# Second mixer of a two-layer language model: gated linear attention with fewer meta outputs, states inside the projection loop, and a head norm by chunk

## What is computed

```python
def gla_chunk(state, q, k, v, log_a):
    cum = jnp.cumsum(log_a, axis=2)
    diff = cum[:, :, :, None, :] - cum[:, :, None, :, :]
    decay = jnp.where(causal[:, :, None], jnp.exp(jnp.minimum(diff, 0.0)), 0.0)
    scores = jnp.einsum('bhtk,bhsk,bhtsk->bhts', q, k, decay)
    out = jnp.einsum('bhts,bhsv->bhtv', scores, v) + jnp.einsum('bhtk,bhkv->bhtv', q * jnp.exp(cum), state)
    last = cum[:, :, -1:, :]
    new_state = state * jnp.exp(last)[:, :, 0, :, None] + jnp.einsum('bhsk,bhsv->bhkv', k * jnp.exp(last - cum), v)
    return new_state, out

def gla_mix(p, g_up, g_b, head_gain):
    q, k, v, gd, r = jnp.split(p, [kw, 2 * kw, 2 * kw + vw, 2 * kw + vw + GLA_LORA], axis=-1)
    log_a = jax.nn.log_sigmoid((gd @ g_up + g_b).astype(f32)) / GLA_TAU   # GLA_TAU = 16
    ...   # 4 heads, keys 128 wide, values 256 wide; one chunk of 16 meta tokens, then 4 chunks of 64
    o = o * lax.rsqrt(jnp.mean(o * o, axis=-1, keepdims=True) + NORM_EPS)
    o = o.reshape(B, T, vw) * head_gain.astype(f32) * jax.nn.silu(r.astype(f32))
    return o.astype(p.dtype)
...
    p = rms_norm(h, o_norm[i]) @ o_w_in[i]
    h = h + gla_mix(p, ...) @ o_w_out[i]
```

## Time and profile before

| What | us |
|---|---|
| Median of 3 runs (lowest, highest) | 939.5 (937.5, 945.36) |
| The profiled execution: its time | 939.7 |
| Its span in the trace | 938.2 |
| PE busy (share) | 807.9 (86%) |
| DVE busy (share) | 342.3 (36%) |
| ACT busy (share) | 195.1 (21%) |
| Mean granted clock of PE | 0.947 |

### The profile page before, as it was taken

How to read it: one execution, slowest core, us unless ns; L and a number is a source line. 1 busy time by engine, 2 the same in 40 slices (tenths; PEclk the granted TensorE clock), 3 DMA queues, 4 the chain that set the end, 5 groups by cost and what they waited for, 6 DMA issues and landing times.

```text
span 938.2 us, 17020 instructions
## 1 busy us (share of the span) xinstructions
PE 807.9 (86%) x7630; PEld 541.1 (58%) x7630; DVE 342.3 (36%) x716; ACT 195.1 (21%) x387; POOL 12.8 (1%) x62
## 2 busy tenths in 40 slices
PE   8999898789999987899889999987899987667765
PEld 6778677764675546455526877866356543334421
DVE  4472756431343332332234065424425221112122
ACT  4552137220500000000012251303031100000002
POOL 5000000000000000000000000000000000000000
PEclk9999899899899999999999999997889998889889
DMA  9451003119649999999998412030564999999994
GB/s 268 131 150 47 1 2 134 50 30 424 266 154 423 420 421 420 368 422 419 422 383 290 158 53 89 1 143 38 222 266 170 422 420 422 420 421 419 421 421 166
DMA packets 61093, 242.06 MB, mean 258 GB/s; under 512 B 9414, under 2 KB 33084, under 8 KB 36060
## 3 DMA queue, kind: packets, MB, share of 16 engines
q1 hardware_dynamic: 60956, 240.94, 65.0%
q10 hardware_dynamic: 64, 0.02, 0.0%
HBM read 239.90 MB, written 1.05 MB: 257 GB/s over the span
## 4 chain that ended last, share of the span: by engine, by line
PE 63%; DMA 24%; DVE 6%; ACT 3%; issue 2%; SPq 1%; PEldq 0%; POOL 0%; DVEq 0%; POOLq 0%
PE ps L1245 11%; DMA M<-in_m_w_down_dram 10%; DMA M<-in_m_w_up_dram 10%; PE ps L790 8%; PE ps L1095 7%; PE ps L989 6%; PE ps L1059 5%; DMA M<-in_m_w_gate_dram 4%; PE ps L1135 4%; PE ps L1072 2%; PE ps L938 2%; PE ps L746 2%; PE ps L1224 1%; PE ps L904 1%; PE ps L1001 1%
## 5 line engine op out<-in xcount | busy, mean ns | idle before, releaser
L1095 PE MATMUL ps<-M 128*32 128x256 f32 x2048 | 127.7, 405 | 45.1 <-DMA M<-in_m_w_gate_dram 33.1
L1095 PEld LDWEIGHTS ps<-M 128*32 128x32 f32 x2048 | 73.0, 117 | 109.4 <-issue 64.2
L1245 PE MATMUL ps<-M 128*128 128x272 f32 (+3 forms) x464 | 108.7, 394 | 1.0 <-DVE M L1349 1.0
L1245 PEld LDWEIGHTS ps<-M 128*128 128x128 f32 (+2 forms) x464 | 82.7, 181 | 23.9 <-issue 4.5
L790 PE MATMUL ps<-M 128*128 128x272 f32 x352 | 88.1, 405 | 1.0 <-DVE M L1349 1.0
L1059 PE MATMUL ps<-M 128*128 128x128 f32 x688 | 81.9, 280 | 3.7 <-DVE M L1727 3.7
L1059 PEld LDWEIGHTS ps<-M 128*128 128x128 f32 x688 | 80.0, 196 | 5.5 <-DVE M L1727 4.6
L1659 DVE TENSOR_TENSOR H<-H,ps 128x512 f32<-128x512 f32 x68 | 46.8, 688 | 87.8 <-PE ps L1072 87.5
L1072 PE MATMUL ps<-M 128*128 128x512 f32 x136 | 68.3, 624 | 9.9 <-DVE H L1662 6.8
L1135 PE MATMUL ps<-M 128*32 128x512 f32 x512 | 65.5, 595 | 13.2 <-DMA M<-in_m_w_down_dram 7.5
L790 PEld LDWEIGHTS ps<-M 128*128 128x128 f32 x352 | 66.5, 193 | 15.9 <-issue 2.0
(11 more groups left out here) (340 smaller groups left out, 864.0 us busy)
## 6 DMA issues: line engine op xcount, KB each, us to landing
M<-in_m_w_gate_dram SPq DMA_DIRECT2D x32, 2048.0 KB, 18.9
M<-in_m_w_up_dram SPq DMA_DIRECT2D x32, 2048.0 KB, 23.5
M<-in_m_w_down_dram SPq DMA_DIRECT2D x32, 2048.0 KB, 25.9
M<-in_o_w_in_dram SPq DMA_DIRECT2D x12, 1024.0 KB, 5.7
M<-in_e_w_in_dram SPq DMA_DIRECT2D x11, 1024.0 KB, 5.2
M<-in_e_w_out_dram SPq DMA_DIRECT2D x1, 4096.0 KB, 14.0
M<-in_o_w_out_dram SPq DMA_DIRECT2D x1, 4096.0 KB, 18.8
H<-in_x_dram SPq DMA_DIRECT2D x2, 512.0 KB, 4.2
```

What stands on the lines that cost most here:

```text
L1095: ins = pe.matmul(ps[32 * e:32 * e + 32, 3 * x, 0:FF], xgT[q % 2][:, k, 32 * e:32 * e + 32], gu_w[UNIT_SLOT[y][u]][:, e, k, :], start=(k = ...
L1245: ins = pe.matmul(ps[rows, unit % 4, 0:n], lhs(k), rhs(k), start=(k == 0), stop=(k == KD - 1))
```

## The change

- **Projection.** The q and r units no longer compute the meta columns (256 instead of 272); k and the decay input keep them. The four value units for the meta tokens become one unit ahead of the other value units: for each of the 8 input blocks four matmuls of 32 weight columns (`xnO` columns 32 to 63) into four strips of 32 partitions, one per value group. It needs the groups 5 to 8 loaded, and ACT evacuates it with four copies of 32 partitions. The 32 rows of `Vo` ahead of them are zeroed. 26 units instead of 29.
- **No meta outputs.** Pairs, exponents, masks and outputs run over chunks 1 to 4; `decayed_rows` over chunks 0 to 3, those that feed a state.
- **States in the loop.** `state_step` stands after units 17, 19, 21 and 23, two steps each; DVE updates them after `pt_add(1)` to `pt_add(4)`. The first state is a copy. The pair rounds stand after units 15, 16, 18, 20, 22, 24 and 25, the exponents after the evacuations 13, 14, 16, 18, 20 and 22.
- **Decay.** min and subtraction are one DVE pass; the factor 1/16 goes into the scale of each Exp.
- **Gate.** ACT multiplies the gain into the gate at its evacuation, a second pass; DVE's eight passes over it go.
- **Head norm by chunk.** ACT squares a chunk's output out of PSUM, PE sums it into four strips of 32 partitions over 64 columns, ACT takes the root of 128x64, DVE inverts it and PE spreads it over the partitions by a column of the identity; DVE multiplies output, gate and spread root into `mixT`. The table of the root is loaded ahead. `mix_part` now counts chunks.
- **Filler.** `keep_busy(4, 5)` and the wait before it go.
- Buffers move to addresses of their own (`wz`), not shown.

```diff
-O_UNITS = [1, 2, 2, 2, 2, 3, 3, 3, 3, 2, 2, 2, 2]
+O_UNITS = [1, 2, 2, 2, 2, 3, 2, 2, 2, 2, 2, 2, 2]
+
+LEVEL_EXP = [13, 14, 16, 18, 20, 22]
+PAIRS_AT = [15, 16, 18, 20, 22, 24, 25]
+STATES_AT = [17, 19, 21, 23]
...
+                elif n == 9:
+                    act.wait_ge(s("pads_zero"), 2)
+                    for g in range(4):
+                        ins = nc.scalar.activation(Vo[32:64, 2, g * 256:(g + 1) * 256], b[32 * g:32 * g + 32, 0:256], ACT.Copy)
...
+                    link(nc.scalar.activation(rr[:, x, META:T], b[:, 0:SEQ], ACT.Silu))
+                    ins = nc.scalar.activation(rr[:, x, META:T], rr[:, x, META:T], ACT.Copy, scale=pcol("gain", x))
...
+            warm_up(ACT.Sqrt)
+
+            def squared(i):
+                act.wait_ge(s("og_done"), i + 1)
+                if i >= 2:
+                    act.wait_ge(s("hs_done"), NC + i - 1)
+                nc.scalar.activation(sqO[i % 2], ps[:, i, :].rearrange("p (x t) -> p x t", x=8), ACT.Square).then_inc(s("cen_sq"), 1)
+
+            def rooted(i):
+                act.wait_ge(s("hs_done"), NC + i + 1)
+                if i >= 2:
+                    act.wait_ge(s("bc_done"), NC + i - 1)
+                nc.scalar.activation(grO[i % 2], ps[:, 4 + i % 2, 0:L], ACT.Sqrt, bias=epsb[:, 0:1], scale=1.0 / 256).then_inc(s("grs"), 1)
+
+            squared(0)
+            for i in range(1, 4):
+                squared(i)
+                rooted(i - 1)
+            rooted(3)
...
-                    pe.wait_ge(s("mix_part"), 2)
-                    keep_busy(4, 5)
                     pe.wait_ge(s("mix_part"), 4)
...
+            def state_step(u):
...
+                if u >= 2:
+                    pe.wait_ge(s("sg_set"), u - 1)
+                for h in (2 * pair, 2 * pair + 1):
+                    ins = pe.matmul(ps[:, 5 + 2 * (u % 2), (h % 2) * 256:(h % 2) * 256 + 256], kdt[r, sl, h, :],
+                                    Vo[r, sl, h * 256:(h + 1) * 256], start=True, stop=True)
+                ins.then_inc(s("sg_done"), 1)
...
+                    t0 = PAD if 3 <= g < 5 else L
+                    todo = [(slice(0, P), TP - t0, lambda k, m=m: wg[:, k, m * P:(m + 1) * P], lambda k, t=t0: xnO[:, k, t:TP])
                             for m in range(2)]
...
+                if g == 5:
+                    todo = [None] + todo
+                    for x in (6, 7, 8):
+                        group_loaded(x)
...
+                            for x in range(4):
+                                ins = pe.matmul(ps[32 * x:32 * x + 32, unit % 4, 0:256], xnO[:, k, 32:64],
+                                                wring[:, (5 + x) % 5, k, :], start=(k == 0), stop=(k == KD - 1))
...
+                    if unit in STATES_AT:
+                        u = 2 * STATES_AT.index(unit)
+                        pe.wait_ge(s("kdt_set"), 1)
+                        pe.wait_ge(s("oproj_evac"), 18 if u else 10)
+                        state_step(u)
+                        state_step(u + 1)
...
+            def summed(i):
+
+                pe.wait_ge(s("cen_sq"), NC + i + 1)
+                if i >= 2:
+                    pe.wait_ge(s("grs"), 2 * NC + 2 * i - 3)
                 for x in range(2):
+                    for h in range(4):
+                        ins = pe.matmul(ps[QUAD[h], 4 + i % 2, 0:L], ones[:, 0:32], sqO[i % 2][:, 2 * h + x], start=(x == 0), stop=(x == 1))
+                ins.then_inc(s("hs_done"), 1)
+
+            def spread_norm(i):
+
+                pe.wait_ge(s("grs"), 2 * NC + 2 * i + 2)
+                if i >= 2:
+                    pe.wait_ge(s("mix_part"), i - 1)
+                for h in range(4):
+                    ins = pe.matmul(ps[:, 6 + i % 2, h * L:(h + 1) * L], ident[:, 32 * h:32 * h + 1].to_broadcast([P, P]), grO[i % 2],
+                                    start=True, stop=True)
+                ins.then_inc(s("bc_done"), 1)
+
+            from_state(1)
+            from_state(2)
+            summed(0)
+            from_state(3)
+            spread_norm(0)
+            summed(1)
+            from_state(4)
+            spread_norm(1)
+            summed(2)
+            spread_norm(2)
+            summed(3)
+            spread_norm(3)
...
-            link(v.tensor_scalar(LA, LA, 0.0, None, ALU.min))
-            link(tt(LA, LA, EA, ALU.subtract))
-            link(v.tensor_scalar(LA, LA, 1.0 / 16, None, ALU.mult))
+            link(stt(out=LA, in0=LA, scalar=0.0, in1=EA, op0=ALU.min, op1=ALU.subtract))
...
+                tt(ocO[i % 2], ps[:, i, :].rearrange("p (x t) -> p x t", x=8), rr[:, :, t0:t0 + L], ALU.mult).then_inc(s("oc_set"), 1)
+                v.wait_ge(s("grs"), 2 * NC + 2 * i + 1)
+                v.reciprocal(grO[i % 2], grO[i % 2]).then_inc(s("grs"), 1)
...
+            scaled(0)
+            for i in range(1, 4):
+                scaled(i)
+                normed_out(i - 1)
+            normed_out(3)
```

More of the change, by code:

```diff
@@ L170, in program, with wz @@
         xnO = arr(19, KD, TP)
[L171 to L182, removed]
+        def wz(first, *dims):
+            n = 1
+            for d in dims:
+                n *= d
+            v = W[:, first:first + n]
+            names = " ".join("abcd"[:len(dims)])
+            return v.rearrange(f"p ({names}) -> p {names}", **{"abcd"[i]: d for i, d in enumerate(dims)}) \
+                if len(dims) > 1 else v
+        qO, kO = wz(0, 4, TP), wz(1280, 4, TP)
+        rr = wz(2560, 8, T)
+        Vo = wz(4736, 3, D)
+        CU, QE, KDc, EA, QH, KH, EB, LA = (wz(b, 4, TP) for b in (8832, 10112, 11392, 12672, 13952, 15232, 17296, 21504))
+        PT, PTt = wz(16512, 2, 4, L), wz(20736, 2, 4, L)
+        gdT = wz(17024, T)[0:16]
+        kdt = wz(19200, 3, 4, P)
+        SG = [None] + [wz(b, 4, FF) for b in (7808, 21504, 22528, 11392)]
+        ocO = [wz(12672 + 512 * i, 8, L) for i in range(2)]
+        sqO = [wz(13952 + 512 * i, 8, L) for i in range(2)]
+        grO = [wz(15232 + L * i, L) for i in range(2)]
         elast = sb("elast", [P, 4, NC])
@@ L620, in _ @@
             entry(1)
-            for n in range(29):
+            for n in range(26):
                 act.wait_ge(s("oproj"), n + 1)
@@ L1204, in decayed_rows @@
                 for h in range(4):
-                    for c in range(NC):
+                    for c in range(NC - 1):
                         sl, half = PLACE[c]
@@ L1250, in _ @@
                         decayed_rows()
-                    if unit >= 15 and unit % 2 == 1 and unit < 29:
-                        pairs((unit - 15) // 2)
+                    if unit in PAIRS_AT:
+                        pairs(PAIRS_AT.index(unit))
+                    if unit in STATES_AT:
[4 more added lines that the diff above has]
+                        state_step(u + 1)
                 if g == 4:
@@ L1287, in _ @@
-            for c in range(NC):
-                pe.wait_ge(s("sg_set"), 4 * c + 1)
+            pe.wait_ge(s("oproj_evac"), 26)
+            pe.wait_ge(s("pt_used"), 8)
+            for cs in ((1, 2), (3, 4)):
+                for h in range(4):
+                    for x in range(2):
+                        for m in range(2):
+                            for d in cs:
+                                sd, hd = PLACE[d]
+                                rd = slice(64 * hd, 64 * hd + 64)
+                                v0 = h * 256 + x * P + 64 * m
+                                pe.matmul(ps[64 * m:64 * m + 64, d - 1, (2 * h + x) * L:(2 * h + x + 1) * L],
+                                          Vo[rd, sd, v0:v0 + 64], PT[rd, sd, h, :],
+                                          start=(h == 0 and x == 0), stop=False,
+                                          skip_group_check=True)
@@ L1747, in _ @@
             entry(1, xnO[:, :, PAD:TP])
[L1749 removed]
+            for x in (kO, EA):
                 v.memset(x[:, :, 0:PAD], 0.0)
[L1751 removed]
+            v.memset(Vo[0:32, 2, :], 0.0)
+            v.wait_ge(s("xn"), 2 * KD)
+            v.memset(LA[:, :, 0:PAD], 0.0)
             link(v.memset(QH, 0.0))
@@ L1821, in _ @@
-            v.wait_ge(s("oproj_evac"), 29)
-            for x in range(8):
-                ins = v.tensor_scalar(rr[:, x], rr[:, x], col("gain", x), None, ALU.mult)
-            link(ins)
-            for h in range(4):
-                v.wait_ge(s("og_act"), 8 + h + 1)
-                link(v.reciprocal(LA[:, h, 0:T], LA[:, h, 0:T]))
-                for x in range(2):
-                    link(tt(rr[:, 2 * h + x], rr[:, 2 * h + x], LA[:, h, 0:T], ALU.mult))
-                    ins = tt(mixT[:, 2 * h + x], oG[:, 2 * h + x, PAD:TP], rr[:, 2 * h + x], ALU.mult)
-                ins.then_inc(s("mix_part"), 1)
+            v.wait_ge(s("oproj_evac"), 26)
```

171 lines of the change are left out of this document (76 added, 95 removed).

## The result

The changed kernel takes 912.01 us (median of 4 runs, 909.94 to 919.14) against 938.57 us: a ratio of 0.9716, 95% interval 0.9643 to 0.9789. The forecast was 912.8 us, range 903 to 922. The profiled execution took 910.19 us with a span of 908.0, two us under the median. As in the prediction, stages are compared between profiled executions.

The account below looks back on a forecast made before the run. Expert weight DMA sets the pace, so the mixer's end sets the time: 34.1 us earlier at full clock, less 6.1 for stall and low clock, less 1.3 at the projection, 26.7 off: 912.8 us, range 903 to 922.

Parts of the forecast that it names:

- Loop: Mixer's projection loop up to unit 26, bound by PE: ends at 614.7 instead of 623.5 us, -8.8 us.
- Tail without the stall, from the products of scores and values on: Mixer after the last evacuation, at full clock: from 615.7 us to its end at 631.9 us.
- Stall: PE waits for instructions near 619 us, behind the dense intra products: one stop of 3.4 us, bounds 0 and two.
- Low clock behind it: After PE's stop, at 1.2 GHz: three output chunks cost +2.3 us and the first broadcast +0.4 us.
- Start of the projection: Output projection behind the mixer, without filler before it, may start at the low clock: +1.3 us, bounds 0 and 2.9.
- From unit 4 to the end: Expert weight stream, 20 units of 4 MB back to back: 220 us as now.
- The cover of the waits: In the loop, DVE's 6.1 us and ACT's at most 6 us per 10.1 us PE round: waits cost nothing.
- The stall's reading: PE's 3.37 us issue stop at 629.65 us in the old kernel, read as waiting for the instruction stream.
- serial ring: Head norm in the tail: root, reciprocal, broadcast product, next summing and hand-overs follow one another, 2.8 us per chunk.
- The outputs that were to lie beside the ring: In the tail, the other two output chunks, 0.93 us each, run beside the norm's serial chain.
- the one without a stall: In the tail, instructions arrive in time: 32.8 us off, 906.7 us; chance 0.25.
- The persistent low clock: Projection and routing behind the mixer run at 1.2 GHz, adding about 46 us: 958 us; chance 0.03.

Follow-up runs that it names:

- unit 0 late, projection early: Changed kernel with unit 0 of the expert weights issued at `mix_part` 4 and two output projection quarters started at `mix_part` 2: 902.39 us, ratio 0.9621.
- one line: Changed kernel with unit 0 of the expert weights issued with unit 1, at `mix_part` 4, instead of at the loop's end: 908.88 us, ratio 0.9673.
- projection early: Changed kernel with the first two output projection quarters started at `mix_part` 2, the last spreading product inside them: 906.61 us, ratio 0.965.

## Why the prediction was right

The time was right, 912.8 against 912.0, and so was the mechanism in the main: a mixer that sets when the stream of expert weights can start, a loop bound by PE, a stall for instructions behind the dense products. Against the profiled execution it was 2.8 us too slow. Term by term:

| Term | forecast | measured |
|---|---|---|
| Loop | -8.8 | -7.7 |
| Tail without the stall, from the products of scores and values on | 16.2 | 15.3; 14.9 with no slow spread (unit 0 late, projection early) |
| Stall | 3.4 | 2.36 |
| Low clock behind it | 2.7 | 0 in three executions, 1.2 and 2.2 in two |
| Start of the projection | +1.3 | +1.6 between unit 1 and unit 4 |
| From unit 4 to the end | 220 | 219.6 |

- The loop term was 1.1 us off, by several small errors. 7.11 us for two adjacent units gave 3.55 for one; a unit that stands between small products takes 3.65, and in the new order all twelve behind the 14th do. So the output gate saved 0.9 us, not 1.8. The decayed rows saved nothing (32 records in 2.77 us, 40 in 2.76 before) where 0.55 was put down. The state steps cost 1.92 a pair, not 1.8; the pair rounds 1.08, not 1.2, which gave 1 us back. The cover of the waits held: no gap before a state step, none in the strip unit (3.59 us).
- The tail was put 0.9 us too long, and its picture was half right. Only the last two rounds are a serial ring, 2.49 us from root to root, where 2.8 was put down. The first two are PE alone: a chunk of outputs (1.08 us, not 0.93), a spread (1.03) and a summing (0.36), 2.47 us together. The outputs that were to lie beside the ring are the chain there, and the two lengths agree by chance.
- The stall's reading was right where it was weakest: the first layer gave no second example, and the row names no cause. Its size was taken over unchanged, which was too much by 1 us, and so was the low clock behind it. That term belongs to single executions, as the ones that had it show.
- Together: loop +1.1, tail -0.9, stall -1.0, low clock -2.7, so the profiled mixer ended at 634.3 us and not at 638.0. That the median lies within 1 us of the forecast is in part luck: errors of both signs, and a median 1.8 us above the profiled execution. The changed kernel's executions spread over 9 us, and no profile shows the longer ones.
- By the Trainium skill, page "Runtime: NRT & Kernel Launch", section "Instruction fetch mechanics", crossing a block of instructions is mostly hidden. The runs agree more or less where no bulk transfer is under way (0.16 and 0.73 us) and don't when 4 MB are in flight beside the dense products (2.36 and 3.37 us).
- Of the rivals, the one without a stall (906.7) was the wrong picture for this kernel. It is what one line makes of it, 908.9. The persistent low clock (958) didn't come: at 640 us the clock was at 1.00 again.

Where the gain comes from, by the runs: the strip unit about 10 us; the norm by chunk without the filler 6.4 us by the medians; and the stall with its low clock, which cost 4.5 us in the kernel before and still costs 3 to 4 here by the medians and ratios (6.9 and 1.7 us of tail in the profiled executions), so anything up to 5 us. The rest of the 26.6 us, 5 to 10, is by subtraction what was not tried alone: meta outputs left out, narrower units, the gate and decay passes. The states' move into the loop gave nothing by itself, and 3 us were lost by it as long as unit 0 went out at the loop's end.

## What to carry to other kernels

Before moving work off the path, look at what is on the DMA engines beside the densest stretch of PE instructions. Here a burst of small products used up instructions faster than they arrived while 4 MB were in flight, and the prefetch, which wasn't needed for another 50 us, could just as well be issued after it. When a serial ring across engines leaves PE in gaps, try to fill them with the part of the next stage whose inputs are ready: here that brought unit 4 5.0 us closer to unit 1, and filler 1.5 us.

## What the runs showed of the hardware

- A packet of PE's instructions started 2.3 us later with a 4 MB transfer under way (621.1 against 618.8 us), and took as long as without it (0.93 and 0.94 us). PE went on 2.2 to 2.6 us behind the start of that packet in all ten executions of the table.
- In the changed kernel PE stopped behind 196 records of the tail: from the start of the packet before, at 607.5 us, to the stall it ran 260 matmul records and 259 weight loads.
- After a gap of 2.3 us the same stream kept PE's clock at 1.00 in two kernels (three executions) and fell to 0.61 in a third (projection early). So what PE does up to the gap, and how long the gap is, didn't settle the clock behind it.
- PE was busy for 2.80 of the last 5.50 us of the tail and began the next stage at 0.50; with filler in the gaps it was busy for 5.40 of 5.40 us and began at 1.00:

```profile
628.80:634.30 5.50, 2.80 (x32) 2.38 (x32) 3.58 (x7) 0.63 (x2) 0.00 (x0) 0.88 0.00 1
628.80:634.20 5.40, 5.40 (x46) 3.02 (x38) 3.56 (x7) 0.63 (x2) 0.00 (x0) 1.00 0.02 5
634.20:655.20 21.00, 21.00 (x51) 9.34 (x51) 1.88 (x5) 0.00 (x0) 0.00 (x0) 1.00 0.96 386
```
